# Two attention phases: half-width maxima items, a third score and output bank, a query copy in four parts, probability sums one step later

## The chip, the cores and the metric

One Trainium2 chip, one core. The time is the device time of one execution in microseconds (us). A kernel is run several times; the median counts, lower is better.

## What is computed

Two layers of a transformer over 2048 tokens and 1024 channels, everything in float32. Each layer is an attention mixer, an output projection, a layernorm of `ALPHA * x + y`, and a gated addition of a projected side input. Cut to what matters here:

```
for i in range(DEPTH):                       # DEPTH = 2
    y = mixers[i % N_MIXERS](x, positions, *layer_params[i]) @ w_out[i]
    x = _layernorm(DEEPNORM_ALPHA * x + y, ln_g[i], ln_b[i])
    x = x + jax.nn.sigmoid(x @ pe_gate[i]) * (p[i] @ pe_proj[i])
# layer 0: 16 heads in 4 groups that share keys and values, window of 128 keys, a sink per head
s = jnp.where(mask, jnp.einsum('bqgrd,bkgd->bgrqk', qblk, kb) * scale, NEG_INF)
pr = jax.nn.softmax(jnp.concatenate([s, snk], -1), axis=-1)[..., :-1]
# layer 1: 16 heads of latent attention, causal over all 2048 keys
s = (einsum(q_nope, k_nope) + einsum(q_rope, k_rope)) * scale
```

The output of a mixer is multiplied by `silu(z)`, its gate.

## The kernel before

The program runs four kinds of phase one after the other: a projection (`gemm_phase`, names `in_`), the windowed attention of layer 0 (`attention_phase`, names `swa_`), a chain of projections (`chain_phase`, names `end_`), the latent attention of layer 1 (`attention_phase` again, names `mla_`), and a last chain. The change is in `attention_phase` and its two configurations, `swa_config` and `mla_config`.

A matrix product is done with operands split into a high and a low part (`ph` and `pl` for probabilities), so a score takes two or three passes and a weighted sum of values two or three.

**Units, steps and chunks.** The work of a phase is a list of units: 8 in the windowed phase (one group of 4 heads and one half of the tokens each), 16 in the latent phase (one head each). A unit is a list of steps (`flat`), one step being one block of 128 keys against up to 512 query columns. The windowed phase has 15 or 16 steps a unit, 124 in all, two to a chunk of output (the first chunk of every other unit has one); the latent phase has 40 a unit, four chunks of 4, 8, 12 and 16 steps. All engines walk the same list of slots `g`, each in its own program order; semaphores join them:

- TensorE (PE): `scored(g)` makes the scores of step g in `score[g % nscore]`; then the maxima products of this slot, `item(v, n)`; then, at slot g, `weigh(g - lag)` adds values times probabilities into an output bank `o_ps[c % 2]`. `lag` is 2 in the windowed phase and 3 in the latent one.
- ScalarE (ACT): `load_gate` (a DMA issue) at a chunk's first step, two exponentials per step (`ph` and `p`), and behind them `denominators(c)` and `store(c)` with their DMA issues. Once a unit, `max_row` issues the DMA of the next unit's row of maxima, and in the windowed phase also an exponential and its store.
- GpSimd (POOL): `pl = p - ph` for each step.
- VectorE (DVE): the maxima of this slot, the running sum of probabilities (`add(g)`, latent phase only), and `out_gate(c)` three slots after the chunk's last step: output bank times gate into `o_out[c % 3]`, for which the store of chunk c - 3 has to have landed.

**Maxima one unit ahead.** The softmax needs each query's maximum before its unit begins, so the products of queries and keys are made once more in the unit before, into two buffers `mx_ps`. An item is what fills one buffer; `share` spreads the next unit's items over slots 0 to 8 (windowed) or 0 to 32 (latent). PE may write item n only when DVE is done with item n - 2:

```
pe.wait_ge(mx_done, item0[u] + n - len(mx_ps) + 1)
```

In the windowed phase an item is one query block of all four heads: 4 products of 256 columns, a buffer of 1024 columns (two of the 8 banks), 8 items a unit. The banks are then 2 scores, 4 for maxima, 2 outputs. In the latent phase an item is one product of up to 512 columns, 40 a unit. When all are reduced, `gather` combines them (slot 9 or 33), PE turns them (`turn`), and DVE negates them (`negate`) two slots later.

**What waits for the output bank.** PE's first `weigh` of chunk c waits until chunk c - 2 is gated. ACT's `load_gate` at the first step of chunk c waits, in the windowed phase, until chunk c - 3 is gated. Both are first due in the same slot.

**Query copy.** In the windowed phase DVE copies a unit's 64x4096 queries into a second tile (`copy_queries`), at slot 5 of the unit before.

**Loads.** SP issues the loads of later units when the last score of a unit is made (`scores` at `ends[...]`): 2 MB of queries, and keys and values, at the turn of each unit.

Of the kernel before, what the change touches and what calls it, by code (L numbers as in the profile page):

```python
# [15 lines left out]
AX = mybir.AxisListType  # L16
# [2046 lines left out]
def attention_phase(nc, consts, name, cfg):  # L2063
# [20 lines left out]
    with ExitStack() as ctx:  # L2084
# [5 lines left out]
        lag, nbuf, nscore = (3, 6, 3) if long else (2, 5, 2)  # L2090
# [38 lines left out]
        o_ps = [s.ps(f"o{b}", [P, TC]) for b in range(2)]  # L2129
# [98 lines left out]
        copy_at = 5  # L2228
# [54 lines left out]
        def _(pe):  # L2283
# [26 lines left out]
            def scored(g):  # L2310
                u, k, st = flat[g]
                if k == 0:
                    pe.wait_ge(ld_b[u % 2], 16 * cfg["n_load_b"] * (u // 2 + 1))
                    pe.wait_ge(*row_landed(0 if lead and u == 0 else last_turn[u]))
                    if not long:
                        pe.wait_ge(q_copied, u + 1)
# [19 lines left out]
            def weigh(g):  # L2336
# [8 lines left out]
                out, high, low = o_ps[c % 2][:, off:TC], p_hi[g % nbuf][:, off:TC], p_lo[g % nbuf][:, off:TC]  # L2345
# [6 lines left out]
            def denominator(c):  # L2352
                pe.wait_ge(summed, adds[last_of[c] + 1])
                pe.wait_ge(sum_ok, c + 1)
                for j in range(TC // P):
                    last = mm(o_ps[c % 2][:, j:j + 1], acc[c % 2][:, j * P:(j + 1) * P], consts["ones"][:, 0:1], True, True)
# [28 lines left out]
        def _(act):  # L2385
# [16 lines left out]
            def low_half(c):  # L2402
# [3 lines left out]
                act.copy(o_low[c % 2][:], o_ps[c % 2][HEAD_DIM:P, :]).then_inc(low_ok, 1)  # L2406

            def denominators(c):
                if long:
                    act.wait_ge(den_ok, c + 1)  # L2410
                    per = TC // P
                    act.copy(den_cols[:, per * c:per * (c + 1)], o_ps[c % 2][:, 0:per]).then_inc(row_ok, 1)  # L2412
# [4 lines left out]
                act.copy(den_row[c % small][:], o_ps[c % 2][HEAD_DIM:HEAD_DIM + 1, :]).then_inc(row_ok, 1)  # L2417
# [57 lines left out]
        def _(dve):  # L2475
            vec = nc.vector
            def item(u, n):
# [5 lines left out]
                out = mx[:].rearrange("p (j n) -> p j n", j=x["groups"])[:, :, x["col"]:x["col"] + 1]  # L2483
                mask = x["products"][0][3]
                if mask is None:
                    op = vec.tensor_reduce(out[:, :, 0], src, AX.X, ALU.max)  # L2486
                else:
                    mt = consts[mask]
                    for j in range(x["groups"]):
                        op = vec.tensor_tensor_reduce(src[:, j, :], src[:, j, :],  # L2490
                                                      mt[:, mt.shape[1] - x["width"]:mt.shape[1]], 1.0, LOWEST,
                                                      ALU.add, ALU.max, out[:, j, :])
# [51 lines left out]
            def copy_queries(u):  # L2544

# [3 lines left out]
                vec.tensor_copy(q_tiles[1][u % 2][0:HEAD_DIM, :], q_tiles[0][u % 3][0:HEAD_DIM, :].bitcast(F32)  # L2549
                                ).then_inc(q_copied, 1)  # L2550

            def finish(c):
# [3 lines left out]
                vec.tensor_tensor(o_sum[c % 2][:], o_ps[c % 2][0:HEAD_DIM, :], o_low[c % 2][:], ALU.add  # L2556
                                  ).then_inc(sum_ok, 1)

            def out_gate(c):
# [4 lines left out]
                vec.tensor_tensor(o_out[c % small][:], o_ps[c % 2][0:HEAD_DIM, :], gate[c % n_gate][:], ALU.mult  # L2564
# [6 lines left out]
            if not long:  # L2571
                copy_queries(0)
# [335 lines left out]
```

## Time and profile before

| | |
|---|---|
| median of 3 runs | 3054.64 us (3053.04 to 3061.67) |
| the profiled execution | 3053.61 us |
| its span, first to last instruction | 3051.8 us |
| TensorE busy | 2892.7 us, 95% |
| VectorE / ScalarE / GpSimd busy | 1938.8 / 1590.5 / 1392.0 us |
| windowed attention, first score to last | 492.5 to 724.7 us |
| latent attention, first maxima product to last | 1685.7 to 2556.4 us, scores on to about 2620 us |

A row of the trace in order of time reads: start in us, duration in us, engine, line, operation, output<-inputs, partitions x elements, count; in brackets the idle time of that engine just before it and what ended it. PEld is TensorE's loading of weights, which overlaps the product before; ACTq and SPq are DMA issues of ScalarE and SyncE. L2285 is the helper that issues every product of an attention phase, so its rows are told apart by their tiles. A product with `const_ident_b` (a mask added to the scores) marks each windowed step.

### The profile page before, as it was taken

The numbers are of one execution on the slowest core, as the hardware profiler recorded it, in microseconds if no ns is written. First come the engines' busy times: TensorE is split into PE (matmuls) and PEld (weight loads), VectorE is DVE, ScalarE is ACT, GpSimd is POOL, SyncE is SP. The second block draws the span as 40 slices with busy tenths as digits, with TensorE's granted clock in tenths as the row PEclk, the third lists the DMA queues.
The fourth block names the chain that finished last, engine by engine and source line by source line (L and its number), as shares of the span: only waits on it lengthen the run. The fifth ranks groups of instructions, "written<-read, shape, count | busy, mean of one in ns | idle before, by whom it ended". The sixth has DMA issues, their size and how long they took to land. (4 is left out here: it accounts for less than half of the span.)

```text
span 3051.8 us, 41224 instructions
## 1 busy us (share of the span) xinstructions
PE 2892.7 (95%) x13411; PEld 2328.4 (76%) x13411; DVE 1938.8 (64%) x3398; ACT 1590.5 (52%) x2808; POOL 1392.0 (46%) x1139
## 2 busy tenths in 40 slices
PE   8999996888999999999998799999999999899998
PEld 6888884566888788777877588888888878688776
DVE  4543315663578864555664588888888887357875
ACT  3111114666445544444544277777777777534643
POOL 0022104665232540001440388888888889423353
PEclk9999997999999999999999699999999999999999
DMA  5343437565997675455799634435335342498674
GB/s 165 84 136 125 117 118 242 179 203 172 308 277 239 201 247 183 159 177 167 251 328 380 148 73 102 103 73 116 91 78 127 73 92 87 157 301 270 212 243 145
DMA packets 284760, 530.13 MB, mean 174 GB/s; under 512 B 29200, under 2 KB 110992, under 8 KB 277392
## 3 DMA queue, kind: packets, MB, share of 16 engines
q1 hardware_dynamic: 218528, 391.22, 43.3%
q10 hardware_dynamic: 66032, 136.48, 14.7%
q8 instruction: 96, 1.57, 0.2%
q14 instruction: 104, 0.85, 0.1%
HBM read 346.85 MB, written 180.49 MB: 173 GB/s over the span
## 5 line engine op out<-in xcount | busy, mean ns | idle before, releaser
L2609 POOL TENSOR_TENSOR mla_pl<-mla_p,mla_ph 128x512 fp32r<-128x512 f32 (+3 forms) x640 | 702.9, 1121 | 144.4 <-ACT mla_p L2458 141.5
L1523 PE MATMUL end_bank<-end_xh,end_whi 128*128 128x512 f32 x1808 | 718.1, 397 | 44.3 <-DVE end_wlo L1754 17.0
L1525 PE MATMUL end_bank<-end_xh,end_wlo 128*128 128x512 f32 x1808 | 708.2, 392 | 0.0
L1524 PE MATMUL end_bank<-end_xl,end_whi 128*128 128x512 f32 x1808 | 707.6, 391 | 0.0
L1592 ACT CAST end_whi<-early_wraw 128x1024 fp32r<-128x1024 f32 (+1 forms) x204 | 211.4, 1036 | 531.8 <-PE end_bank L1525 510.7
L2457 ACT ACTIVATE mla_ph<-mla_score 128x512 fp32r<-128x512 f32 (+3 forms) x640 | 342.4, 535 | 238.0 <-PE mla_score L2285 232.9
L1754 DVE TENSOR_TENSOR end_wlo<-early_wraw,end_whi 128x1024 fp32r<-128x1024 f32 x188 | 255.4, 1358 | 317.9 <-ACT end_whi L1592 317.7
L1523 PEld LDWEIGHTS end_bank<-end_xh,end_whi 128*128 128x128 f32 x1808 | 342.1, 189 | 134.9 <-DVE end_wlo L1754 24.6
L2542 DVE TENSOR_TENSOR mla_acc<-mla_acc,mla_p 128x512 f32<-128x512 f32 (+3 forms) x576 | 351.0, 609 | 106.6 <-ACT mla_p L2458 104.2
L1524 PEld LDWEIGHTS end_bank<-end_xl,end_whi 128*128 128x128 f32 x1808 | 342.3, 189 | 72.6 <-issue 2.9
L1525 PEld LDWEIGHTS end_bank<-end_xh,end_wlo 128*128 128x128 f32 x1808 | 341.6, 189 | 72.4
L2458 ACT ACTIVATE mla_p<-mla_score 128x512 f32<-128x512 f32 (+3 forms) x640 | 338.4, 529 | 0.0
L2285 PE MATMUL mla_score<-mla_q,mla_k 96*128 96x512 f32 (+7 forms) x1200 | 331.5, 378 | 0.0
L2486 DVE TENSOR_REDUCE mla_mx<-mla_mx 128x1 f32<-128x512 f32 x384 | 258.8, 685 | 45.4 <-PE mla_mx L2285 44.9
L2285 PEld LDWEIGHTS mla_score<-mla_q,mla_k 96*128 96x128 f32 (+1 forms) x1200 | 222.1, 191 | 35.5
L907 PE MATMUL in_bank<-in_xh,in_whi 128*128 128x512 f32 x576 | 225.8, 392 | 14.1 <-DVE in_xl L740 14.1
L2285 PE MATMUL mla_o<-mla_pl,mla_v 128*128 128x512 f32 (+3 forms) x640 | 237.4, 371 | 1.8 <-POOL mla_pl L2609 1.5
L2285 PE MATMUL mla_o<-mla_ph,mla_v 128*128 128x512 f32 (+3 forms) x640 | 237.2, 371 | 1.3 <-ACT mla_den_cols L2412 0.3
L909 PE MATMUL in_bank<-in_xl,in_whi 128*128 128x512 f32 x576 | 225.1, 391 | 0.0
L911 PE MATMUL in_bank<-in_xh,in_wlo 128*128 128x512 f32 x576 | 225.1, 391 | 0.0
L2609 POOL TENSOR_TENSOR swa_pl<-swa_p,swa_ph 128x512 fp32r<-128x512 f32 x124 | 165.6, 1347 | 93.5 <-ACT swa_p L2458 90.8
L1020 POOL TENSOR_TENSOR in_ta<-in_ta,in_tb 128x512 f32<-128x512 f32 x20 | 25.9, 1294 | 273.0 <-DVE in_tb L808 273.0
(242 smaller groups left out, 4985.7 us busy)
## 6 DMA issues: line engine op xcount, KB each, us to landing
early_wraw<-in_pe_gate ACTq DMA_DIRECT2D x64, 512.0 KB, 4.9
early_wraw<-in_w_out ACTq DMA_DIRECT2D x62, 512.0 KB, 7.3
early_wraw<-in_w_in ACTq DMA_DIRECT2D x56, 512.0 KB, 3.8
scratch_q<-in_rope SPq DMA_DIRECT2D x64, 256.0 KB, 2.9
swa_q<-scratch_q SPq DMA_DIRECT2D x8, 2048.0 KB, 9.2
end_factor<-scratch_inv SPq DMA_DIRECT2D x64, 256.0 KB, 9.6
scratch_proj<-end_out_f SPq DMA_DIRECT2D x64, 256.0 KB, 6.9
scratch_sum<-end_out_f SPq DMA_DIRECT2D x64, 256.0 KB, 6.3
```

The source lines that it names most:

```text
L907: nc.tensor.matmul(banks[b][t][:], w_hi[b][:, at], hi[b][:, k, tok], start=(k == 0), stop=False)
L909: nc.tensor.matmul(banks[b][t][:], w_hi[b][:, at], lo[b][:, k, tok], start=False, stop=False)
L1523: nc.tensor.matmul(bank, wh[:, at], xh[:, k0 + k * nq, :], start=(k == 0), stop=False)
L1524: nc.tensor.matmul(bank, wh[:, at], xl[:, k0 + k * nq, :], start=False, stop=False)
L1525: last = nc.tensor.matmul(bank, wl[:, at], xh[:, k0 + k * nq, :], start=False, stop=(k == kc - 1))
L1754: vec.tensor_tensor(w_lo[b % n_w][:], w_raw[b % n_raw][:], w_hi[b % n_w][:].bitcast(F32), ALU.subtract).then_inc(w_lo_ok, 1)
L2285: return nc.tensor.matmul(out, lhs, rhs, start=start, stop=stop)
L2457: act.activation(p_hi[b][:, off:TC], bank[:, off:TC], ACT.Exp, scale=scale)
L2458: act.activation(prob[b][:, off:TC], bank[:, off:TC], ACT.Exp, scale=scale).then_inc(probs, 1)
L2486: op = vec.tensor_reduce(out[:, :, 0], src, AX.X, ALU.max)
L2542: vec.tensor_tensor(into[:, both], acc_ps[:, both], now[:, both], ALU.add).then_inc(summed, 1)
L2609: pool.tensor_tensor(p_lo[b][:, off:TC], prob[b][:, off:TC], p_hi[b][:, off:TC].bitcast(F32), ALU.subtract).then_inc(p_lo_ok, 1)
```

## The change

- Windowed phase: an item of maxima is now two heads of a query block (2 products, one bank of 512 columns), 16 items a unit; `share` spreads them over the same slots 0 to 8, one, two or three to a slot. Two banks hold maxima, 3 scores, 3 outputs. PE's first `weigh` of chunk c waits for chunk c - 3 to be gated.
- Windowed phase: the query copy is 4 copies of 64x1024, at slots 9, 10, 12 and 13; all four before the unit's first score.
- Latent phase: DVE adds step g - 1 in slot g, behind the maxima of slot g; a chunk's last step is still added in its own slot. Banks are as before.

```diff
-        lag, nbuf, nscore = (3, 6, 3) if long else (2, 5, 2)
+        lag, nbuf, n_o = (3, 6, 2) if long else (2, 5, 3)
+        nscore = 3
...
-        copy_at = 5
+        copy_at = (9, 10, 12, 13)
+        q_parts = len(copy_at)
...
-                if st["first"] and c >= 2:
-                    pe.wait_ge(row_ok, c - 1)
+                if st["first"] and c >= n_o:
+                    pe.wait_ge(row_ok, c - n_o + 1)
                     if not long:
-                        pe.wait_ge(gated, c - 1)
+                        pe.wait_ge(gated, c - n_o + 1)
...
-                    if not long and k == copy_at and u + 1 < units:
-                        copy_queries(u + 1)
+                    if not long and k in copy_at and u + 1 < units:
+                        copy_queries(u + 1, copy_at.index(k))
                     for v, n in at_slot(u, k):
                         item(v, n)
-                    add(g)
+                    if not st["first"]:
+                        add(g - 1)
+                    if st["last"]:
+                        add(g)
...
-            it.append(dict(products=[(j * half_b * P + c * P, blks[0][0] * P, width, "window_q", j * 2 * P)
-                                     for j in range(GROUP)],
-                           stride=2 * P, groups=GROUP, width=width, col=c))
+            for j0 in range(0, GROUP, 2):
+                it.append(dict(products=[((j0 + j) * half_b * P + c * P, blks[0][0] * P, width, "window_q", j * 2 * P)
+                                         for j in range(2)],
+                               stride=2 * P, groups=2, width=width, col=j0 * half_b + c, per=half_b))
...
-                max_cols=half_b * GROUP, max_width=2 * TC, items_to=8, long=False,
+                max_cols=half_b * GROUP, max_width=TC, items_to=8, long=False,
```

The rest of the diff follows from these: `% 2` becomes `% n_o` where an output bank is named, and the columns of `mx` are sliced for two heads.

How the order moves, on VectorE at the end of the first windowed unit. Before, between the last maxima and the next unit's first (`swa_m_all` is the gathering, `swa_m_t` the negating, `swa_o_out` a gate):

```order
L2490 ISA swa_mx 128x1
L2509 SCALAR_TENSOR_TENSOR swa_m_all<-swa_sink_q,swa_mx 128x32
L2564 TENSOR_TENSOR swa_o_out<-swa_o,swa_gate 64x512
L2522 TENSOR_SCALAR swa_m_t<-swa_mx 32x128
L2564 TENSOR_TENSOR swa_o_out<-swa_o,swa_gate 64x512 x2
L2490 ISA swa_mx<-swa_mx,const_window_q 128x128
```

and now:

```order
L2492 ISA swa_mx 128x1
L2551 CAST swa_q<-swa_q 64x1024
L2511 SCALAR_TENSOR_TENSOR swa_m_all<-swa_sink_q,swa_mx 128x32
L2566 TENSOR_TENSOR swa_o_out<-swa_o,swa_gate 64x512
L2551 CAST swa_q<-swa_q 64x1024
L2524 TENSOR_SCALAR swa_m_t<-swa_mx 32x128
L2566 TENSOR_TENSOR swa_o_out<-swa_o,swa_gate 64x512
L2551 CAST swa_q<-swa_q 64x1024 x2
L2566 TENSOR_TENSOR swa_o_out<-swa_o,swa_gate 64x512
L2492 ISA swa_mx<-swa_mx,const_window_q 128x128
```

The four copies stand around the gathering and the negating; the 64x4096 copy that stood among the maxima is gone from there. One copy is now in front of the gathering.

On TensorE in the same unit, slots 2 and 3 before:

```order
L2285 MATMUL swa_mx<-swa_k,swa_q 128x256 x4
L2285 MATMUL swa_o<-swa_ph,swa_v 128x512 x2
L2285 MATMUL swa_o<-swa_pl,swa_v 128x512
L2285 MATMUL swa_score<-swa_q,swa_k 128x512
L2285 MATMUL swa_score<-const_prev_t,const_ident_b 128x512
L2285 MATMUL swa_score<-swa_q,swa_k 128x512
L2285 MATMUL swa_mx<-swa_k,swa_q 128x256 x4
```

and now:

```order
L2287 MATMUL swa_mx<-swa_k,swa_q 128x256 x2
L2287 MATMUL swa_o<-swa_ph,swa_v 128x512 x2
L2287 MATMUL swa_o<-swa_pl,swa_v 128x512
L2287 MATMUL swa_score<-swa_q,swa_k 128x512
L2287 MATMUL swa_score<-const_prev_t,const_ident_b 128x512
L2287 MATMUL swa_score<-swa_q,swa_k 128x512
L2287 MATMUL swa_mx<-swa_k,swa_q 128x256 x4
```

Slot 2 has one half-width item now; x4 is two of them, with a wait ahead of each. The products of maxima stand in front of the products of values (`swa_o`) in every slot.

On VectorE in the latent phase, second chunk of a head, before and now:

```order
L2542 TENSOR_TENSOR mla_acc<-mla_acc,mla_p 128x384
L2490 ISA mla_mx<-mla_mx,const_causal_q 128x384
L2490 ISA mla_mx 128x1
L2542 TENSOR_TENSOR mla_acc<-mla_acc,mla_p 128x256
L2486 TENSOR_REDUCE mla_mx<-mla_mx 128x1
L2542 TENSOR_TENSOR mla_acc<-mla_acc,mla_p 128x128
L2556 TENSOR_TENSOR mla_o_sum<-mla_o,mla_o_low 64x512
```

```order
L2492 ISA mla_mx<-mla_mx,const_causal_q 128x384
L2492 ISA mla_mx 128x1
L2544 TENSOR_TENSOR mla_acc<-mla_acc,mla_p 128x384
L2488 TENSOR_REDUCE mla_mx<-mla_mx 128x1
L2544 TENSOR_TENSOR mla_acc<-mla_acc,mla_p 128x256
L2558 TENSOR_TENSOR mla_o_sum<-mla_o,mla_o_low 64x512
```

Each addition (`mla_acc`) stands one slot later against the maxima (`mla_mx`) and against `mla_o_sum`.

## Rows read from the trace of the kernel before

**Rows 1.** The page, busy time by engine.

```profile
PE 2892.7 (95%) x13411; PEld 2328.4 (76%) x13411; DVE 1938.8 (64%) x3398; ACT 1590.5 (52%) x2808; POOL 1392.0 (46%) x1139
```

**Rows 2.** Busy time by stretch: windowed, latent; then granted clock, DMA share, GB/s.

```profile
550.00:580.00 30.00, 26.38 (x124) 18.13 (x123) 20.09 (x75) 19.95 (x38) 19.15 (x15) 1.00 0.70 207
...
2040.00:2140.00 100.00, 98.54 (x522) 80.82 (x520) 81.70 (x184) 76.22 (x167) 87.27 (x80) 1.00 0.47 103
```

**Rows 3.** Mask products of windowed steps in order of time; each marks a step.

```profile
550.32 0.39 PE L2285 MATMUL swa_score<-const_causal_t,const_ident_b 128*128 128x512 bf16 x1
552.18 0.39 PE L2285 MATMUL swa_score<-const_prev_t,const_ident_b 128*128 128x512 bf16 x1
...
703.67 0.39 PE L2285 MATMUL swa_score<-const_prev_t,const_ident_b 128*128 128x512 bf16 x1
...
724.68 0.39 PE L2285 MATMUL swa_score<-const_causal_t,const_ident_b 128*128 128x512 bf16 x1
```

**Rows 4.** Maxima before a first score: windowed (four-head items), the copy's waiter, latent (one bank).

```profile
479.92 1.23 PE L2285 MATMUL swa_mx<-swa_k,swa_q 128*128 128x256 f32 x4 [0.31 <-DVE swa_mx L2490]
...
492.46 0.76 PE L2285 MATMUL swa_score<-swa_q,swa_k 128*128 128x512 f32 x1 [2.75 <-DVE swa_q L2549]
...
1691.17 1.12 PE L2285 MATMUL mla_mx<-early_k,early_q 96*128 96x512 f32 x2 [0.57 <-DVE mla_mx L2486]
```

**Rows 5.** TensorE's waits, 480 to 735 us: total, times, longest.

```profile
PE swa_o L2285 <- DVE swa_o_out L2564: 13.7, 15, 1.5
PE swa_score L2285 <- ACT swa_p L2458: 5.4, 6, 1.1
```

**Rows 6.** Third windowed unit: its loads, a store, and who waits.

```profile
549.38 0.58 SPq L2237 DMA_DIRECT2D swa_q<-scratch_q  x1
...
551.72 0.61 ACTq L2433 DMA_DIRECT2D scratch_o<-swa_o_out  x1
...
561.35 0.68 DVE L2564 TENSOR_TENSOR swa_o_out<-swa_o,swa_gate 64x512 f32<-64x512 f32 x1 [2.44 <-DMA scratch_o<-swa_o_out]
...
562.18 0.70 PE L2285 MATMUL swa_o<-swa_ph,swa_v 128*128 128x512 f32 x2 [1.16 <-DVE swa_o_out L2564]
```

**Rows 7.** VectorE's waits for stores, whole windowed phase.

```profile
DVE swa_o_out L2564 <- DMA scratch_o<-swa_o_out: 18.5, 10, 3.1
```

**Rows 8.** A query copy, and GpSimd and TensorE beside it.

```profile
531.86 2.27 DVE L2549 CAST swa_q<-swa_q 64x4096 fp32r<-64x4096 f32 x1
532.02 3.25 POOL L2609 TENSOR_TENSOR swa_pl<-swa_p,swa_ph 128x512 fp32r<-128x512 f32 x1 [0.69 <-ACT swa_p L2458]
...
535.33 0.50 PE L2285 MATMUL swa_o<-swa_pl,swa_v 128*128 128x512 f32 x1 [0.66 <-POOL swa_pl L2609]
```

**Rows 9.** End of the second windowed unit.

```profile
548.39 0.50 PE L2285 MATMUL swa_score<-swa_q,swa_k 128*128 128x512 f32 x1 [0.94 <-ACT swa_p L2458]
...
549.75 0.19 PEld L2285 LDWEIGHTS swa_o<-swa_pl,swa_v 128*128 128x128 f32 x1 [0.37 <-POOL swa_pl L2609]
```

**Rows 10.** TensorE late for VectorE: third step of a unit, slot 10, slot 8.

```profile
557.52 0.70 PE L2285 MATMUL swa_o<-swa_ph,swa_v 128*128 128x512 f32 x2 [0.49 <-DVE swa_o_out L2564]
...
540.50 0.70 PE L2285 MATMUL swa_o<-swa_ph,swa_v 128*128 128x512 f32 x2 [0.58 <-DVE swa_o_out L2564]
...
661.56 0.62 PE L2285 MATMUL swa_mx<-swa_k,swa_q 128*128 128x256 f32 x3 [1.27 <-DVE swa_mx L2490]
```

**Rows 11.** Waits in one latent head, 2343.6 to 2399.5 us, and its first.

```profile
PEld mla_mx L2285 <- DVE mla_mx L2490: 0.8, 1, 0.8
PEld mla_mx L2285 <- DVE mla_mx L2486: 0.6, 3, 0.3
PEld mla_mx L2308 <- DVE mla_m_all L2504: 0.3, 1, 0.3
...
DVE mla_acc L2542 <- ACT mla_p L2458: 5.5, 17, 0.7
...
2343.64 0.44 PE L2285 MATMUL mla_mx<-early_k,early_q 96*128 96x384 f32 x1 [0.64 <-DVE mla_mx L2490]
```

More of the change, by code:

```diff
@@ L2128, in attention_phase @@
         mx_ps = [s.ps(f"mx{b}", [P, mx_w]) for b in range(2)]
-        o_ps = [s.ps(f"o{b}", [P, TC]) for b in range(2)]
+        o_ps = [s.ps(f"o{b}", [P, TC]) for b in range(n_o)]
         acc_ps = s.ps("acc", [P, TC]) if long else None
@@ L2315, in scored @@
                     if not long:
[L2316 removed]
+                        pe.wait_ge(q_copied, q_parts * (u + 1))
                 if lead and u == 0 and st["first"] and st["chunk"] * (TC // P) == lead["blocks"]:
@@ L2405, in low_half @@
                     act.wait_ge(sum_ok, c - 1)
-                act.copy(o_low[c % 2][:], o_ps[c % 2][HEAD_DIM:P, :]).then_inc(low_ok, 1)
+                act.copy(o_low[c % 2][:], o_ps[c % n_o][HEAD_DIM:P, :]).then_inc(low_ok, 1)
             def denominators(c):
@@ L2411, in denominators @@
                     per = TC // P
-                    act.copy(den_cols[:, per * c:per * (c + 1)], o_ps[c % 2][:, 0:per]).then_inc(row_ok, 1)
+                    act.copy(den_cols[:, per * c:per * (c + 1)], o_ps[c % n_o][:, 0:per]).then_inc(row_ok, 1)
                     return
@@ L2482, in item @@
                 src = mx_ps[n % len(mx_ps)][:].rearrange("p (j k) -> p j k", k=x["stride"])[:, 0:x["groups"], 0:x["width"]]
-                out = mx[:].rearrange("p (j n) -> p j n", j=x["groups"])[:, :, x["col"]:x["col"] + 1]
+                out = [mx[:, col:col + 1] for col in range(x["col"], n_mx, x["per"])[0:x["groups"]]]
                 mask = x["products"][0][3]
                 if mask is None:
-                    op = vec.tensor_reduce(out[:, :, 0], src, AX.X, ALU.max)
+                    op = vec.tensor_reduce(out[0], src, AX.X, ALU.max)
                 else:
@@ L2491, in item @@
                                                       mt[:, mt.shape[1] - x["width"]:mt.shape[1]], 1.0, LOWEST,
-                                                      ALU.add, ALU.max, out[:, j, :])
+                                                      ALU.add, ALU.max, out[j])
                 op.then_inc(mx_done, 1)
@@ L2542, in add, with copy_queries @@
                 vec.tensor_tensor(into[:, both], acc_ps[:, both], now[:, both], ALU.add).then_inc(summed, 1)
-            def copy_queries(u):
+            def copy_queries(u, part):
+                mine = slice(part * qw // q_parts, (part + 1) * qw // q_parts)
                 if u >= 2:
@@ L2571, in _ @@
             if not long:
-                copy_queries(0)
+                for part in range(q_parts):
+                    copy_queries(0, part)
             for g in range(total + tail):
@@ L2699, in mla_config @@
                 items.append(dict(products=[(i * P, kc * TC, width, mask, 0)], stride=TC, groups=1,
-                                  width=width, col=len(items)))
+                                  width=width, col=len(items), per=1))
     def load(u, q_tile, k_tile, part):
```

12 lines of the change are left out of this document (6 added, 6 removed).

## The prediction

> **What bounds the kernel now.** I read the page first: TensorE is busy 95% of the span and nothing else comes near it [rows 1], so a change pays only where TensorE stands. Then the stretches, to see where it stands. In the latent phase it is busy 98.5 of 100 us; in the windowed phase 26.4 of 30 us, at full granted clock in both [rows 2]. Windowed attention is where there is something to win, latent attention where little is left per us but the phase is long.
>
> How much the windowed phase stands idle I take from its steps, because the ends of products are modelled and step starts are not. The last unit, which makes no maxima, runs from 703.67 to 724.68: 15 steps in 21.01 us, 1.40 each. With a four-head item of maxima a step takes 552.18 - 550.32 = 1.86 us, so an item costs 0.46. The phase has 123 intervals and 56 items after its first step: 123 x 1.40 + 56 x 0.46 = 198 us [rows 3]. It takes 724.68 us less the start of the first score, 492.46 [rows 4], 232.2 us, of which 0.6 lie before the first mask. So 33 us are stalls, 14%.
>
> The list of waits names them in part: 15 times the first product of a chunk's values waits for the gate of the chunk two before (13.7 us), 6 times a score waits for ScalarE (5.4 us) [rows 5]. Behind them are three causes:
>
> - **Stores held by loads.** At the turn of a unit the 2 MB query load and its fellows start (549.38). A store issued at 551.72 is what the gate at 561.35 waits for, so it took 9.6 us. The gate then ends at 562.03 and TensorE, which had stood 1.16 us, goes on at 562.18 [rows 6]. VectorE is held like this 10 times, 18.5 us in all [rows 7].
> - **The query copy.** It takes VectorE 2.27 us in slot 5, among the maxima. In the slots 0 to 8 VectorE has an item of 1.54 us (the pace of the items before the first score, 1.23 + 0.31 [rows 4]) and on average half a gate of 0.68 [rows 6], 1.88 us a slot, just what TensorE's slot takes. So it can't catch up before slot 9. The same copy stops GpSimd: a subtraction that began 0.16 us after the copy took 3.25 us, and TensorE waited 0.66 us for it [rows 8].
> - **The unit's end.** ScalarE has three or four DMA issues and the sink's exponential in slot 12 and comes to step 13 late. A score then waits 0.94 us for a free bank, and next the low part of the values waits for GpSimd until 549.75 [rows 9].
>
> **The change, part by part** (sum against the profiled execution, 3053.61 us; the median of the runs is 1.0 above it).
>
> *Third score bank.* At the unit's end the score that started at 548.39 can start about 1 us earlier. But the values of step 13 still need its probabilities and GpSimd's low part, so TensorE gets past this place at 549.75 as before [rows 9]: 0.1 us won. In the other four units the score that waits is the next unit's first, and the maxima behind it, 0.46 us of work, move into the gap. 4 x 0.46 + 3 x 0.1, about **-2.0**. Bounds: 0 and -5.4, the whole wait [rows 5].
>
> *Query copy in four parts behind the maxima.* What VectorE loses in slot 5 no longer reaches slots 6 to 10. TensorE stands 0.6 us at slot 10 in three units and, once, 1.3 at slot 8 [rows 10]; with the weight loads ahead of these products, and with the subtractions that the copy stopped (0.66 [rows 8] and a smaller one), that is **-5.0**; bounds 0 and -8. The parts cost VectorE about 7 x 4 x 0.57 (a quarter of 2.27) where it is idle after slot 9; one stands ahead of the gathering, which has over a slot of slack to the turn in slot 11. At the phase's beginning TensorE waits for the whole copy, 2.75 us [rows 4]; four instructions for one can only make that longer, +0.2. No row shows a 64x1024 copy; I bound it by 0.57 below and by the 0.68 of a gate above.
> By the Trainium skill, "VectorE: DVE Perf Modes", the errata section, each such instruction pays a fixed cost of 58 cycles, 0.06 us at 0.96 GHz; by it the beginning would be 0.18 us longer. The same skill's "GPSIMD Engine Reference", Key points, says that GpSimd shares its SBUF interfaces with VectorE; rows 8 show that as a full stop for one copy's length, and by that rule the four parts hold GpSimd just as long in all, only never over 0.6 us at once.
>
> *Third output bank.* The wait of the values for the gate of chunk c - 2 goes. ScalarE's gate load still waits for chunk c - 3, due in the same slot as the old wait; but TensorE needs the step behind it two slots later, after some 3 us of its own work, so that is covered while a hold is under 2 us. Late gates whose removal nothing replaces: one in the fourth slot of four units (0.49 and the weight load ahead, 0.7 each [rows 10]) and, at the end of unit 6, where no maxima follow, one of the longest (1.5 [rows 5]): **-4.4**.
>
> *Maxima in one bank.* This is what was paid for the banks. An item may be written when VectorE is done with the item two before; that was two slots back, and is now one slot back, since a slot has two items. At 561.35 VectorE stands in front of a gate. The maxima of the next slot lie behind it. TensorE, one slot on, needs the first of these before it may write: 562.03 + 0.77 = 562.80, and the second 0.77 later, and the products of maxima stand in front of the values. So the old wait (to 562.18) becomes a new one to about 562.8 and 563.5 in the same slot. Between 0.6 and 1.4 us more per hold, less the slots that have one item; 10 holds, from 0 to +15, I take 0.6 each: **+6**. Slots are tighter elsewhere too, but VectorE's two items (1.54 us) fit in a slot.
> At the phase's start, with no scores between, four-head items go at VectorE's pace, 1.54 us, with TensorE 1.23 us at work and 0.31 waiting [rows 4]. Half the size leaves the same waits against half the work: per pair of half items 0.3 + 0.7 + 0.77 = 1.77 against 1.54, over 7 pairs **+1.6**. The latent phase, whose items are of one bank, shows such a wait of 0.57 us for two products [rows 4].
>
> *Latent sums one slot later.* VectorE waits 5.5 us a head for probabilities in front of additions, and the maxima behind them start late. Weight loads of TensorE wait for maxima 0.6 us and for the gathering 0.3 us a head [rows 11]; now neither stands behind a wait of this slot. Part of such a gap is hidden by the product before, whose own row shows no idle time; from the starts I read 0.5 us lost of the 0.9. 15 heads: **-7.5**, bounds 0 and -13.5. The wait of 0.84 at each head's begin (0.64 of TensorE itself) stays, since a chunk's last step is still added in its own slot and the first items of the next head stand behind that. The sums have 6 slots to the denominator; nothing is late by that.
>
> Sum: -2.0 - 5.0 + 0.2 - 4.4 + 6 + 1.6 - 7.5 = -11.1. 3053.6 - 11.1 = 3042.5, say **3042**: 0.4% faster.
>
> **The rivals.**
> *The banks win what they aim at.* The loads start up to 1 us earlier in three units, as the last score no longer waits, and what VectorE saves lets it take a hold. If holds no longer reach TensorE, 20 of the 33 us go: 3053.6 - 20 - 7.5 = 3026. Against it: the held gate is fixed by a store's landing, and TensorE's next items hang on VectorE.
> *Nothing to measure.* The latent weight loads were hidden and the windowed terms cancel: 3050, anything within 9 us of now. For it: latent product rows show idle time only at a head's begin [rows 11].
> *The tight maxima decide.* Slower: every hold costs both half items (+15), and the half items outside the start lose 0.14 us each by the back and forth between TensorE and VectorE (112 x 0.14 = +16), with all gains as above but the latent one: 3053.6 + 15 + 16 + 1.8 - 11.4 = 3075; with the latent gain 3067. It decides as soon as VectorE is a slot late in slots 0 to 8, and its load there equals TensorE's. Against it: in a slot TensorE has 1.4 us of scores and values to cover a half item's 0.77.
>
> **How the numbers follow.** A measurement of this kernel tells about 0.3%, 9 us, from no change. My forecast 0.45 (own range 3034 to 3050; four fifths of it over 0.3% faster), the banks win 0.22, nothing to measure 0.23, tight maxima 0.10. Faster 0.36 + 0.22 = 0.58, same 0.09 + 0.22 = 0.31, slower 0.10 + 0.01 = 0.11. The range of eight in ten goes from 3024 to 3058: it takes in the banks' case and leaves out the slower one.
>
> **What would show it.** Right: waits of values for a gate nearly gone, new waits of `swa_mx` products for VectorE's maxima of 0.6 us or more behind held gates; holds by stores still about 10; windowed steps in 225 to 230 us; a latent head in about 55.4 us where it took 55.9, with its first wait of 0.64 still there; no subtraction of 3 us on GpSimd. Wrong: windowed steps under 215 us (then holds don't reach TensorE), or over 235 us; a latent head unchanged.

## The result, and the profile after

| | before | changed |
|---|---|---|
| median | 3053.86 us (3053.04 to 3061.67, 4 runs) | 3084.18 us (3082.20 to 3090.80, 4 runs) |
| the profiled execution, its span | 3053.61, 3051.8 us | 3084.33, 3082.5 us |
| VectorE waits for stores, windowed | 18.5 us in 10 | 27.9 us in 13 |
| windowed steps, first mask to last | 231.65 us | 241.04 us |
| a latent head | 55.9 us | 56.7 us in nine, 58.3 us in five |

The change made the kernel slower by 1.0%, ratio 1.0097 (95% interval 1.0075 to 1.012). The forecast was 3042 us, faster, with a range from 3024 to 3058. By stages, from the starts in the two traces, the 30.7 us of the span come from:

- 2.6 us ahead of the windowed phase: its first product starts at 478.71 and not at 476.08. No edit touches what lies before it; over all kernels run here this start lay between 476.0 and 480.2. It is not the change's.
- 1.6 us from there to the first mask product (18.53 against 16.95).
- 9.4 us in the windowed steps, 497.24 to 738.28 against 493.03 to 724.68. One trace of each kernel shows this size only roughly: five traces of the changed windowed code have a mean of 239.8 us for the steps, and two of the code before 233.7, which is about 6 us more.
- -1.6 us in the chain between the two attentions.
- 17.3 us in the latent phase, from the issue of its first row of maxima to that of its last: 883.64 against 866.37. The first two intervals are 2.0 shorter; then nine heads take 0.83 us more each and five 2.37, 19.3 us together. The 2.0 can't be put down to the change: eight other traces with each addition in its own slot took 81.3 to 83.9 us for these two intervals, the changed kernel 81.7 and the kernel before 83.8.
- 1.4 us behind it.

The stretches that [rows 2] show, in the changed kernel. In the windowed one TensorE is busy 24.0 of 30 us instead of 26.4, and the granted clock (third figure from the end; 1.00 is 2.4 GHz, 0.50 is 1.2 GHz) is 0.94 instead of 1.00; in the latent one it is busy 98.3 of 100 us, with a clock of 0.98:

```profile
550.00:580.00 30.00, 24.00 (x104) 15.99 (x103) 16.97 (x69) 17.26 (x33) 16.52 (x14) 0.94 0.65 196
2040.00:2140.00 100.00, 98.30 (x493) 79.43 (x492) 81.17 (x178) 74.68 (x159) 86.14 (x77) 0.98 0.33 76
```

The list of waits over the windowed steps (engine and line, what it waited for, us in total, times, longest). It answers to [rows 5] and [rows 7]: the 13.7 us for a gate and the 5.4 for ScalarE are gone, and 22.0 for VectorE's maxima have come. VectorE stands longer in front of gates whose output buffer a store still holds (a hold, from here on), up to 5.3 us at once:

```profile
DVE swa_o_out L2566 <- DMA scratch_o<-swa_o_out: 27.9, 13, 5.3
PE swa_mx L2287 <- DVE swa_mx L2492: 22.0, 20, 4.9
PE swa_score L2287 <- DVE swa_q L2551: 2.9, 1, 2.9
```

One place in order of time, the third unit, as in [rows 6]. The store issued at 557.11, 3.4 us behind the 2 MB load of queries (553.70), is what the gate at 569.77 waits for: 12.7 us. The maxima of the next items are read behind that gate, TensorE may not write the next item before, and its values stand behind that product. It stands 4.38 us, and when it goes on its clock falls to half:

```profile
557.11 0.61 ACTq L2435 DMA_DIRECT2D scratch_o<-swa_o_out  x1
...
569.77 0.68 DVE L2566 TENSOR_TENSOR swa_o_out<-swa_o,swa_gate 64x512 f32<-64x512 f32 x1 [4.79 <-DMA scratch_o<-swa_o_out]
570.38 0.41 DVE L2492 CUSTOM_DVE_ANT_0 swa_mx<-swa_mx,const_window_q 128x256 f32<-128x256 f32 x1
...
571.29 1.56 PE L2287 MATMUL swa_mx<-swa_k,swa_q 128*128 128x256 f32 x4 [4.38 <-DVE swa_mx L2492]
```

```profile
568.00:570.00 2.00, 0.00 (x0) 0.00 (x0) 0.23 (x1) 0.00 (x0) 0.20 (x1) 1.00 1.01 358
570.00:572.00 2.00, 0.71 (x2) 0.45 (x2) 2.00 (x9) 0.94 (x2) 0.00 (x0) 0.84 0.68 211
572.00:574.00 2.00, 1.99 (x7) 1.59 (x6) 1.93 (x9) 0.72 (x2) 1.28 (x1) 0.50 0.43 113
```

(Columns: stretch, length, busy time of PE, PEld, DVE, ACT, POOL, then granted clock, DMA share, GB/s.) The step takes 8.07 us where most take about 2, and one in the fifth unit takes 8.55 us in the same way.

In the latent phase, by one head in the place of [rows 11] (2309.8 to 2366.6 us), VectorE waits for probabilities 3.4 us in 8 places instead of 5.5 in 17, as was meant. But it waits for maxima products instead, and over the whole phase the two trade places: 66.9 us for probabilities (104.2 before) and, in the group of unmasked maxima, 88.0 for products (44.9 before). From the page's groups after:

```profile
L2544 DVE TENSOR_TENSOR mla_acc<-mla_acc,mla_p 128x512 f32<-128x512 f32 (+3 forms) x576 | 351.0, 609 | 73.2 <-ACT mla_p L2460 66.9
L2488 DVE TENSOR_REDUCE mla_mx<-mla_mx 128x1 f32<-128x512 f32 x384 | 259.1, 686 | 89.9 <-PE mla_mx L2287 88.0
```

Where TensorE loses it, the same place in a head before and after, from a head's fifth slot on. Before, the addition lies in a gap of 1.37 us between two maxima of VectorE; it is done 0.41 us before the products of the next maxima are:

```profile
2015.80 0.57 DVE L2542 TENSOR_TENSOR mla_acc<-mla_acc,mla_p 128x384 f32<-128x384 f32 x1 [0.39 <-ACT mla_p L2458]
2016.78 0.69 DVE L2486 TENSOR_REDUCE mla_mx<-mla_mx 128x1 f32<-128x512 f32 x1 [0.41 <-PE mla_mx L2285]
```

After: slot 3, the last of the first chunk, ends with the late addition of slot 2, a copy and its own addition, where before only the copy and its own addition stood. The masked maxima behind them come late, and TensorE's weight load waits 0.39 us for them. Then the gap of 1.36 us stands empty and two additions follow the maxima:

```profile
2028.36 0.42 DVE L2544 TENSOR_TENSOR mla_acc<-mla_acc,mla_p 128x256 f32<-128x256 f32 x1
2028.88 0.56 DVE L2543 COPY mla_acc<-mla_acc 128x384 f32<-128x384 f32 x1
2029.35 0.28 DVE L2544 TENSOR_TENSOR mla_acc<-mla_acc,mla_p 128x128 f32<-128x128 f32 x1
...
2030.54 0.19 PEld L2287 LDWEIGHTS mla_mx<-early_k,early_q 96*128 96x128 f32 x1 [0.39 <-DVE mla_mx L2492]
...
2032.82 0.69 DVE L2488 TENSOR_REDUCE mla_mx<-mla_mx 128x1 f32<-128x512 f32 x1 [1.36 <-PE mla_mx L2287]
2033.42 1.09 DVE L2544 TENSOR_TENSOR mla_acc<-mla_acc,mla_p 128x384 f32<-128x384 f32 x2
```

In the head 115 us later the same stall (2145.54) is followed, 2.8 us later, by half the clock for 3.4 us:

```profile
2146.00:2148.00 2.00, 2.00 (x19) 1.91 (x17) 0.64 (x4) 0.82 (x4) 2.00 (x3) 1.00 1.05 233
2148.00:2152.00 4.00, 3.92 (x14) 3.25 (x14) 2.79 (x7) 2.37 (x7) 1.78 (x3) 0.57 1.03 197
```

From the starts of the exponentials, the 0.83 us of a head are lost at its sixth step (0.41), at the one or two behind the second chunk's end (0.3) and behind the third's (0.29), with 0.1 won back in between. In the five longer heads another 1.5 us go at the steps under the lowered clock.

### The profile page after: what moved, and what is told of

Same layout as the page of the kernel before. It is cut to its first block and busy times, and to the rows that moved or that the text cites. A ratio compares the mean times of both kernels' runs of the same rounds, so it can differ in the third digit from the quotient of the medians.

```text
span 3082.5 us, 41265 instructions
## 1 busy us (share of the span) xinstructions
PE 2916.3 (95%) x13411; PEld 2340.7 (76%) x13411; DVE 1946.8 (63%) x3422; ACT 1593.1 (52%) x2808; POOL 1389.5 (45%) x1139
## 5 line engine op out<-in xcount | busy, mean ns | idle before, releaser
L1523 PE MATMUL end_bank<-end_xh,end_whi 128*128 128x512 f32 x1808 | 718.0, 397 | 43.6 <-DVE end_wlo L1754 17.3
L2544 DVE TENSOR_TENSOR mla_acc<-mla_acc,mla_p 128x512 f32<-128x512 f32 (+3 forms) x576 | 351.0, 609 | 73.2 <-ACT mla_p L2460 66.9
L2492 DVE CUSTOM_DVE_ANT_0 mla_mx<-mla_mx,const_causal_q 128x128 f32<-128x128 f32 (+3 forms) x256 | 125.5, 495 | 42.1 <-PE mla_mx L2287 39.8
```

The source lines that it names most:

```text
L1523: nc.tensor.matmul(bank, wh[:, at], xh[:, k0 + k * nq, :], start=(k == 0), stop=False)
L2544: vec.tensor_tensor(into[:, both], acc_ps[:, both], now[:, both], ALU.add).then_inc(summed, 1)
```

## The experiments

Times beside the kernel before are ratios from runs on one chip. "Steps" are the windowed steps, first mask product to last, and "heads" the latent intervals, each from that run's one trace; the steps of one kernel differ by a few us from trace to trace, since the holds do (231.65 and 235.65 us in two traces of the windowed code before, 237.1 to 241.6 in five of the changed code). With six output buffers, where nothing is held, three traces of the same windowed code lie within 1.1 us of each other (211.6 to 212.7). Experiments are edits of the changed kernel unless said otherwise.

### The two parts apart

The kernel before with the late additions alone:

```diff
-                    add(g)
+                    if not st["first"]:
+                        add(g - 1)
+                    if st["last"]:
+                        add(g)
```

> The kernel before with only the latent additions moved one slot later; nothing of windowed attention is changed. Theory A (the 18 us that the latent phase lost come from this edit alone: a chunk's last slot now holds two additions, the maxima of the next slot come late, TensorE stands 0.4 us there three times a head and in some heads its clock falls behind one of these stalls): latent heads of 56.7 us, some of 58.2, the phase about 18 us longer than before, 3072 us (3068 to 3075). Rival A1 (the heads are longer because of something that the windowed edits leave behind, a bank's place or the phase that loads run in): heads of 55.9 or less, 3046 to 3055 us.

Measured 1.006 (1.0037 to 1.0083), 3080.5 us; heads 56.7 us in most and 58.3 in four. The time is above the 3068 to 3075 that were expected, but the kernel before, too, took 3060.0 us on this chip and not 3053.9.

And the changed kernel with that edit undone:

> The changed kernel with each addition back in its own slot: only the windowed edits are left. Theory A: every latent head takes 55.9 us again and the time is 3084 - 18 = 3066 us (3062 to 3070), with windowed steps of 241 us as in the changed kernel. Rival A1: latent heads stay at 56.7 and more, 3080 us or over.

Measured 1.0028 (1.0016 to 1.0041), 3067.8 us, heads 55.9 us, steps 240.2. The two losses are separate: the additions cost the latent phase 15 us (the first run) to 17 us (changed kernel) whatever the windowed code is, the windowed edits the rest. By the medians the additions alone cost 20.5 us and the windowed edits alone 7.8, together 28.3 of the changed kernel's 30.3. A1 is out. The 7.8 also fit the 6 us of the mean steps and the 1.6 of the phase's start.

### Held stores taken away

```diff
-        small, n_gate = 3, 3 if long else 5
+        small, n_gate = (3, 3) if long else (6, 5)
...
+        o_tile = [s.sb(f"o_out{b}", [HEAD_DIM if long else HEAD_DIM + 1, TC]) for b in range(small)]
+        o_out = [t[0:HEAD_DIM, :] for t in o_tile]
+        den_row = None if long else [t[HEAD_DIM:HEAD_DIM + 1, :] for t in o_tile]
```

> The changed kernel with six buffers for gated outputs in windowed attention where it has three (the row of denominators lies in each one's 65th partition, which makes the room), so a gate waits for the store of six chunks ago. Theory B (what the windowed phase lost are stores held by the query loads: VectorE stands in front of a gate for them, the maxima behind it come late, and with banks for one slot only TensorE stands too): VectorE's 27.9 us of waits for stores go to under 3 us, the waits of TensorE for maxima from 23.8 to under 8 us, the two steps of 8 us vanish, and the steps take 215 to 225 us instead of 241: 3084 - 20 = 3064 us (3058 to 3068). Rival B1 (VectorE's load is the limit, and the products of maxima and their reading take turns anyway): the waits for stores go, but the steps stay over 234 us, 3077 us or more.

Measured 0.9993 (0.998 to 1.0006), 3057.4 us, with the latent phase still as slow as in the changed kernel (heads of 56.7 us, and six of 58.3). The waits for stores are gone from VectorE's gates and TensorE's waits for maxima fell from 22.0 us to 1.4. The steps went from 241.0 to 211.7 us, 29 us, more than was expected: the half clock after the two long stalls is gone too, and the longest steps left are six at the units' turns, 2.7 to 2.8 us each. The mask products that bound the steps, and the two waits:

```profile
494.79 0.65 PE L2287 MATMUL swa_score<-const_causal_t,const_ident_b 128*128 128x512 bf16 x1
...
706.48 0.39 PE L2287 MATMUL swa_score<-const_causal_t,const_ident_b 128*128 128x512 bf16 x1
```

```profile
L2566 DVE TENSOR_TENSOR swa_o_out<-swa_o,swa_gate 64x512 f32<-64x512 f32 x64 | 43.4, 677 | 21.1 <-PE swa_o L2287 21.0
...
PE swa_mx L2287 <- DVE swa_mx L2492: 1.4, 3, 0.5
```

The same with the additions in their own slot:

> The changed kernel with six output buffers and with each latent addition in its own slot again. Both losses found so far are taken out, and if they are separate they add: latent heads of 55.9 us (phase about 866 us), windowed steps of about 212 us: 3057.4 - 17 = 3040 us (3036 to 3046) beside 3060 for the kernel before, 0.6% faster. Rival C1 (the shorter windowed phase only moves a wait into what follows, loads of the next phase above all): 3050 us or more.

Measured 0.9948 (0.9935 to 0.9962), 3040.1 us, steps 212.7, heads 55.9. The two repairs add.

The kernel before with six output buffers and nothing else:

> The kernel before with six output buffers in windowed attention and nothing else. Theory D (held stores were nearly all of what the windowed phase could lose, and the banks of the change only move where a hold is felt): its 18.5 us of VectorE waiting for stores go and the steps take 231.7 - 15 to 20 = 212 to 217 us, 3041 to 3048 us, within 4 us of the changed windowed code with six buffers. Rival D1 (the change's third banks, half items and split copy are worth something once nothing is held): steps of 220 us or more here against 212 there, 3050 us or more.

Measured 0.9942 (0.9929 to 0.9956), 3038.4 us, steps 216.3. Theory D holds: without held stores, the code before needs none of the change to be as fast as with it.

And with the late split copy:

> The kernel before with six output buffers and with the query copy in four parts in slots 9, 10, 12 and 13; four-head items and banks as before. If the late split copy is worth what the prediction gave it (5 us), the steps are 5 us shorter than with six buffers alone and GpSimd has no subtraction of over 2 us; if the copy in slot 5 was hidden behind the slack of two slots, they are within 1 us of each other.

Measured 0.9948 (0.9932 to 0.9964), steps 211.3 us, 5.0 less than with six buffers alone, and GpSimd's subtractions take at most 1.77 us each, where seven took 2.86 to 2.97. With four-head items and the old banks this takes no longer than the change's banks with six buffers (211.7, 212.7): third banks and half items are worth nothing once nothing is held. The 5.0 us, from one trace each, don't show in the times, whose interval is 4 to 5 us to either side: the three kernels of 3038 to 3040 us, all of which beat both the kernel before and the changed one, can't be told apart.

### Banks, items and the copy, with stores held

Four banks for maxima, two for scores, two for outputs; items and copy as changed, additions in their own slot:

```diff
-        lag, nbuf, n_o = (3, 6, 2) if long else (2, 5, 3)
-        nscore = 3
+        lag, nbuf, n_o = (3, 6, 2) if long else (2, 5, 2)
+        nscore, n_mx_ps = (3, 2) if long else (2, 4)
```

> The changed windowed code (two-head items, split copy, latent additions in their own slot), three output buffers, but with PSUM shared as before: two score banks, two output banks and four single banks for maxima, so that an item may be written when the one four before (two slots) is read. Theory B (with stores held, what costs is the slack of the maxima, one slot against two): TensorE's waits for maxima go from 23.8 us to under 8, waits for a gate come back, steps of 226 to 232 us where two maxima banks took 240: 3068 - 10 = 3058 us (3053 to 3062). Rival B2 (the two-head items themselves, or the longer holds of the stores, are the loss): steps of 236 us or more.

Measured 1.0004 (0.9989 to 1.002), steps 233.4 us: 1.4 above what was expected, 6.8 below the 240.2 with two maxima banks. The stores hold VectorE nearly as long, 23.8 us against 23.9 in the trace with two banks; what is gone is TensorE's wait for maxima, and the gates' wait is back at its old size:

```profile
DVE swa_o_out L2566 <- DMA scratch_o<-swa_o_out: 23.8, 14, 3.6
PE swa_o L2287 <- DVE swa_o_out L2566: 13.8, 16, 1.9
PE swa_score L2287 <- ACT swa_p L2460: 5.1, 7, 1.0
```

With three score, two output and three maxima banks (`nscore, n_mx_ps = (3, 3)`):

> As the run with four maxima banks, but with three score, two output and three maxima banks. By theory B it lies between: slack of one and a half slots, steps of 230 to 236 us. If the third score bank is what the windowed phase wants, it is the better of the two: under 228 us. If the number of maxima banks does not matter, both take what two banks took, 240 us.

Measured 1.0021 (1.0007 to 1.0035), 3063.8 us, steps 236.3 us, just above the 230 to 236 that were expected, with two steps of 7.0 and 7.9 us. The third score bank is not worth a maxima bank. With 2, 3 and 4 maxima banks the steps take 240.2, 236.3 and 233.4 us and the ratios are 1.0028, 1.0021 and 1.0004; the order is the one that theory B asks for, and four banks are clear of two (237.1 to 241.6 us in five traces), but three are not clear of either: their steps differ from both by no more than the steps of one kernel do, and the intervals overlap. The three runs differ in score and output banks as well, so the slack alone was not varied.

The copy whole, in slot 5 (`copy_at = (5,)`), everything else as in the run of the windowed edits alone:

> The changed windowed code with two maxima banks and the latent additions in their own slot, but the query copy whole and in slot 5 as before. In the kernels with six output buffers the late split copy was worth 5.0 us. Theory B says that with one slot of slack a copy of 2.3 us in front of the maxima costs more than there: steps of 246 to 252 us where they took 240, and GpSimd's subtraction of about 3 us is back. Rival: the copy falls into the time in which VectorE is held for a store anyway, and the steps stay within 2 us of 240.

Measured 1.0066 (1.0046 to 1.0086), 3076.9 us, steps 253.8 us, 13.5 more than with the late split copy and a little over what was expected; the ratios are 0.0038 apart, 12 us. GpSimd's subtractions of 2.6 to 3.1 us are back, seven of them. The clock falls to half at six stalls of 2.0 to 5.8 us here, where it fell at three.

The kernel before with the late split copy alone:

> The kernel before with the query copy in four parts in slots 9, 10, 12 and 13 and nothing else; stores are held as before. By the prediction's own term, steps of 231.7 - 5 = 227 us, 3052 to 3055 us beside 3057 to 3060. Rival: an earlier, freer VectorE only reaches the held stores sooner, and the steps stay over 230 us.

Measured 1.0011 (0.9999 to 1.0024), steps 230.95 us against 231.65, with 23.6 us of VectorE waiting for stores instead of 18.5. The rival is right: the steps stay over 230 us, a gain of 5 us lies outside the interval, and VectorE stands 5.1 us longer in front of held stores. The same edit is worth 0.7, 5.0 and 13.5 us of steps in three surroundings; the first is less than traces of one kernel differ by, and only the last shows in the times.

### The latent additions

The first of the two additions ahead of the last slot's maxima:

```diff
+                    if st["last"]:
+                        add(g - 1)
                     for v, n in at_slot(u, k):
                         item(v, n)
-                    if not st["first"]:
+                    if not st["first"] and not st["last"]:
                         add(g - 1)
```

> The changed kernel, but in a chunk's last slot the addition of the slot before stands ahead of that slot's maxima and not behind them; its probabilities are long there, so it waits for nothing. Theory A in its narrow form (the two additions in a row behind the last slot's maxima are what makes the next maxima late): the stalls of 0.4 us and the clock's falls go, latent heads take 55.4 to 55.9 us, 3062 to 3069 us. Rival A2 (it is the load of that slot on VectorE, wherever the addition stands in it, or the additions' being later as such): heads of 56.5 us or more, 3080 us or over.

Measured 1.0049 (1.003 to 1.0069), 3074.3 us: heads of 56.4 us, none over 56.8. The stall at the sixth step is gone, and with it every fall of the clock in these heads, but 0.5 us a head stay, at the steps behind the second and the third chunk. The narrow form explains part.

The rest is two additions in a row again, now ahead of the last slot's maxima. In the second chunk of a head, before and in this run: one addition, then the maxima; two additions, then the maxima 0.5 us later in the head, for which TensorE's weight load waits:

```profile
2191.18 0.70 DVE L2542 TENSOR_TENSOR mla_acc<-mla_acc,mla_p 128x512 f32<-128x512 f32 x1 [0.20 <-ACT mla_p L2458]
2191.79 0.68 DVE L2486 TENSOR_REDUCE mla_mx<-mla_mx 128x1 f32<-128x512 f32 x1
```

```profile
2204.20 1.49 DVE L2544 TENSOR_TENSOR mla_acc<-mla_acc,mla_p 128x512 f32<-128x512 f32 x2
2205.60 0.68 DVE L2488 TENSOR_REDUCE mla_mx<-mla_mx 128x1 f32<-128x512 f32 x1
...
2206.34 0.19 PEld L2287 LDWEIGHTS mla_mx<-early_k,early_q 96*128 96x128 f32 x1 [0.55 <-DVE mla_mx L2488]
```

Caught up one slot before the chunk's last, with six output buffers (`if st["last"] or flat[g + 1][2]["last"]: add(g)`):

> Six output buffers and the latent additions one slot late, but caught up in the slot before a chunk's last one (two additions there), so that the last slot has one addition as in the kernel before. Theory A2 (what hurts is VectorE's load in a chunk's last slot, in front of the short diagonal steps of the next chunk): the losses at the steps after slots 3, 11 and 23 go, heads take 55.4 to 55.9 us, 3036 to 3041 us. Rival A3 (two additions in one slot hurt wherever they stand, or being one slot late does): heads of 56.3 us or more, 3047 us or over.

Measured 0.9961 (0.9948 to 0.9975), 3044.9 us, heads of 56.4 us again, 56.8 once. But this run is no second test: an addition at the end of one slot and the same addition at the beginning of the next are one place in VectorE's program. In the traces of this run and of the run with the first addition early, VectorE's 1633 instructions of the latent phase stand in the same order, and the heads lose the same time at the same steps. So it repeats that run with six output buffers, and does not decide between A2 and A3. What both runs show is that the loss follows two additions in a row, on whichever side of the last slot's maxima they stand: 0.83 us a head behind them, 0.5 ahead of them. At the other steps, where additions are late one at a time, the heads lose nothing in sum. Whether additions that are late and never caught up in pairs would be free is open; no run has them.

Late additions in a head's first chunk only, and then in all but the first:

```diff
+                    late_sum = st["chunk"] == 0
+                    if not late_sum:
+                        add(g)
-                    if not st["first"]:
+                    if late_sum and not st["first"]:
                         add(g - 1)
-                    if st["last"]:
+                    if late_sum and st["last"]:
                         add(g)
```

> The changed kernel with additions one slot late only in a latent head's first chunk (slots 0 to 3, the short diagonal steps, with the copy of 384 columns in the last); the other three chunks add in their own slot. Theory F (TensorE's clock falls because of the 0.4 us that this chunk's double addition makes it stand among short steps, at the sixth step of a head): heads of 55.9 + 0.4 = 56.3 us, and some of them 1.5 us longer, 57.8, with a granted clock of 0.5 for about 3 us behind the seventh step. Rival F1 (the falls need the losses of the later chunks too, or come from something else in the changed kernel): no head over 56.4 us.

One execution, 3077.4 us beside 3059.2 for the kernel before. Heads of 56.3 us, and three of 57.8. Each of the three has the clock's fall; the stall and the stretch that follows it in the first of them:

```profile
1859.06 0.19 PEld L2287 LDWEIGHTS mla_mx<-early_k,early_q 96*128 96x128 f32 x1 [0.39 <-DVE mla_mx L2492]
```

```profile
1856.00:1860.00 4.00, 3.87 (x23) 2.92 (x23) 3.63 (x11) 3.37 (x8) 2.32 (x4) 1.00 0.99 213
1860.00:1864.00 4.00, 3.93 (x21) 3.33 (x21) 2.54 (x5) 1.74 (x6) 3.31 (x5) 0.74 1.01 223
1864.00:1868.00 4.00, 4.00 (x22) 3.55 (x21) 3.04 (x7) 2.17 (x4) 2.36 (x2) 0.84 1.03 210
```

> The counterpart: additions one slot late in the second to fourth chunk of each head, in their own slot in the first. Theory F: no stall at the sixth step and no fall of the clock in any head, heads of 55.9 + 0.4 to 0.6 = 56.3 to 56.5 us. Rival F1: heads of 58 us among them still.

One execution, 3072.7 us. Heads of 56.3 to 56.4 us, none longer. Theory F holds on both sides: behind the stall of 0.4 us at the sixth step, where the short steps of the first and second chunk meet, the clock can fall; behind the stalls of the later chunks it did not. Over all traces: in the four with this stall (the changed kernel, the additions alone, six output buffers, and the first chunk alone) it fell in 5, 4, 6 and 3 of 14 heads, 18 of 56; in the twelve without, in none of 168. Why it falls in some heads and not in the others, whose steps up to there have the same times, isn't settled. Nor is the last head, which makes no maxima: there TensorE waits 0.42 us for ScalarE near the sixth step in all sixteen traces, and the clock fell in two of them, the run of the additions alone and the one of the first chunk alone. So a stall of this length at this place goes with the falls, whoever causes it, but is not enough for one.

## Why the prediction was wrong

**Latent sums, -7.5 us, measured +17 (19.3 in the fourteen full heads).** This step failed in kind. It took VectorE's 5.5 us a head of waiting for probabilities as time lost to the maxima behind, and said that of TensorE's waits for maxima half would go. The traces show the opposite order: VectorE waited for probabilities where the next maxima's products were not there either, so the addition lay in a gap that nobody paid for. One slot later the gap is empty and the work stands in pairs at a chunk's end, ahead of short steps. "The sums have 6 slots to the denominator; nothing is late by that" looked only at who waits for the sums; late were the maxima queued behind them. The bound of 0 on that side was wrong for the same reason. The first wait of 0.64 us stays, as said (2310.57 in the trace after).

**The clock.** The forecast had no term for it. In the latent phase it is 5 times 1.5 us. In the windowed steps it fell at the two long stalls, for some 10 us of half clock in all; the trace of the kernel before has none there, but the second trace of its windowed code has 7 us, at steps of 4.5 and 5.0 us.

**Maxima in one bank, +6 at ten holds.** The mechanism is the one that was forecast: values no longer wait for a gate, maxima products do, in the same slots. The size failed. Together with the two third banks the prediction had the exchange at -0.4 (-2.0 - 4.4 + 6; the -4.4 is 4.3 when its own parts are added up, 4 x 0.7 + 1.5); two maxima banks and the two third banks against four maxima banks measure +6.8, one trace each, and 7 us by the two ratios. "0.6 each" took a hold as TensorE meets it in [rows 6], where VectorE comes to the held gate with TensorE a slot of work ahead. With one slot of slack a long hold (4.8 and 5.3 us, none before over 3.1) reaches TensorE nearly whole: of the 4.79 us at 569.77 it stands 4.38, where in [rows 6] it stood 1.16 of 2.44. The rival of the tight maxima had the right place and sign, and a chance of 0.10.

**Query copy, -5.0.** The size is met where no store holds VectorE, which is not the case that was forecast. In the kernel before, with its held stores, it is 0.7 us: the time won was spent in front of them. Among the other windowed edits, with one slot of slack, it is 13.5. No single term stands for it, and that one of the three meets the forecast is luck: the prediction summed the terms as if they were independent, though they stand on one engine in a row. That no subtraction of GpSimd takes 3 us any more holds; the longest takes 1.84. The bounds for a 64x1024 copy, 0.57 and 0.68 us, don't hold: it takes 0.67 to 0.68 us where it starts with no subtraction of GpSimd under way, as at the phase's start, but up to 1.77 where one is, 1.19 in the mean of the 28 copies behind the first four. So the parts cost VectorE 33 us and not 16, where the seven whole copies had cost 18:

```profile
547.87 1.70 DVE L2551 CAST swa_q<-swa_q 64x1024 fp32r<-64x1024 f32 x1
```

Half items and split copy cost 1.6 us at the phase's start against 1.8 forecast. By the Trainium skill, "VectorE: DVE Perf Modes", the errata section, four copies for one cost an estimated 0.18 us more in fixed parts (three times 58 cycles). The trace agrees: at the phase's start the four take 2.48 us from the first's start to the last's end (494.05 to 496.53) and the whole one took 2.27, and TensorE's wait went from 2.75 to 2.87 us.

**Half items, nothing outside the start.** With four banks they are 2.4 us slower than four-head items (233.4 against 230.95 with the same copy), which is within what one trace differs from another: nothing or a little.

**What stood in the profile and was not weighed enough.** The prediction named stores held by loads as the first cause, 18.5 us on VectorE [rows 7]; the change had nothing against them, and 20 of the 33 us were called reachable by the banks. Taking the holds away was worth 15 us in the kernel before and 29 in the changed one.

## What to carry to other kernels

An engine's wait is only worth removing if the work behind it could have run: look at what that engine waits for next. If moving the wait lets it reach a second wait, the work that filled the gap is merely late. Moving an instruction from the end of one step to the beginning of the next changes nothing where the engine has nothing in between; compare the order of the instructions before taking two runs for two tests. Slack in a ring of buffers is what keeps a hold on one engine from becoming a stall on another; before taking buffers from one ring for another, find the longest hold, and take away its cause first. Gains from two edits on one engine's queue don't add while that queue is held by something else.

## What was not expected of the hardware

A store of 128 KB issued among the loads of a unit's turn, 2 MB of queries first, took 12.7 us from issue to the gate that it freed, in [rows 6] 9.6; the median of all such stores in the changed kernel is 2.6 us to landing. TensorE's granted clock fell to half after it had stood 4.4 us, and the half clock lasted 3.4 us. In the latent phase it fell to half for 3.4 us behind a stall of only 0.4 us, among short products and with eight products of a single column (0.95 us together) right behind the stall, in 18 of 56 heads over four traces, though TensorE was busy 9.79 of the 10 us around (2142 to 2152). In the twelve traces without that stall it did not fall between the end of the phase's first 60 us and its last exponential. A copy on VectorE and a subtraction on GpSimd hold each other up: the subtraction took 3.25 us instead of 1.27 beside a long copy [rows 8], and a short copy up to 1.77 instead of 0.68 beside a subtraction.
